# Four RMS norms of a transformer kernel: VectorE adds up the squares, and TensorE's ones product runs on the total

## What the kernel computes

```python
def _rmsnorm(x, g):
    xf = x.astype(jnp.float32)
    y = xf * lax.rsqrt(jnp.mean(xf * xf, -1, keepdims=True) + EPS) * g.astype(jnp.float32)
    return y.astype(x.dtype)

D_MODEL = 1024
SEQ = 512
FFN_HIDDEN = -(-8 * D_MODEL // (3 * 256)) * 256     # 2816
```

## Time and profile before

| | |
|---|---|
| median of 3 runs (lowest, highest) | 3064.34 us (3064.19, 3064.74) |
| span of the profiled execution, first to last instruction | 3059.0 us |
| TensorE busy | 2888.6 us, 94% of the span |
| VectorE busy | 792.2 us, 26% |
| ScalarE busy | 498.4 us, 16% |
| mean granted TensorE clock | 0.974 of full speed |

### The profile page before, as it was taken

The page is one execution under the profiler, slowest core; times in us unless marked ns, Lnnn a source line. Parts: engine busy times, 40 slices in busy tenths (PEclk is TensorE's granted clock), DMA queues, the critical chain, the costliest instruction groups (busy, mean ns, idle before and its releaser), DMA issues. The chain is left out here.

```text
span 3059.0 us, 31313 instructions
## 1 busy us (share of the span) xinstructions
PE 2888.6 (94%) x13580; PEld 1501.2 (49%) x13580; DVE 792.2 (26%) x1577; ACT 498.4 (16%) x1045; POOL 101.0 (3%) x90
## 2 busy tenths in 40 slices
PE   7998999999999999999998999789969989996998
PEld 4343475444455447544446745788623334432332
DVE  2325531010003233000002274555221231112113
ACT  2333310000001231000001231443110010001001
POOL 1000000000010010000000200010000000000000
PEclk9999999999999999999999999998989999997999
DMA  7211036545221111222111201100099953009994
GB/s 244 93 42 42 28 115 262 218 180 220 82 85 69 68 66 56 87 78 83 69 69 60 111 29 59 34 23 2 23 399 419 419 207 145 14 6 395 419 420 193
DMA packets 68577, 430.81 MB, mean 141 GB/s; under 512 B 8042, under 2 KB 8857, under 8 KB 21464
## 3 DMA queue, kind: packets, MB, share of 16 engines
q1 hardware_dynamic: 63640, 412.48, 34.5%
q0 software_dynamic: 4800, 16.33, 1.5%
HBM read 422.33 MB, written 13.79 MB: 143 GB/s over the span
## 5 line engine op out<-in xcount | busy, mean ns | idle before, releaser
L295 PE MATMUL bank<-h,weight_ring 128*128 128x512 f32 (+1 forms) x1600 | 608.3, 542 | 0.0
L295 PEld LDWEIGHTS bank<-h,weight_ring 128*128 128x128 f32 x1600 | 303.1, 190 | 300.3 <-issue 290.4
L254 PE MATMUL bank<-arena,weight_ring 128*128 128x512 f32 (+1 forms) x1264 | 422.9, 491 | 0.0
L254 PEld LDWEIGHTS bank<-arena,weight_ring 128*128 128x128 f32 x1264 | 238.1, 190 | 170.5 <-issue 154.5
L2151 PE MATMUL bank<-weight_ring,tokens_T 128*64 128x512 f32 x1024 | 231.8, 603 | 1.5 <-issue 1.5
L906 PE MATMUL bank<-h,weight_ring 128*128 128x512 f32 (+2 forms) x464 | 183.1, 547 | 5.2 <-DVE h L202 3.4
L2638 PE MATMUL bank<-h,weight_ring 128*128 128x256 f32 (+1 forms) x576 | 172.9, 457 | 8.5 <-ACT h L1933 8.5
L309 DVE TENSOR_TENSOR arena<-bank,arena 128x512 f32<-128x512 f32 (+1 forms) x50 | 31.4, 627 | 557.3 <-ACT arena L304 557.3
L3286 PE MATMUL bank<-h,weight_ring 128*128 128x512 f32 x384 | 166.6, 597 | 3.7 <-DMA weight_ring<-in_sc_in 3.7
L2151 PEld LDWEIGHTS bank<-weight_ring,tokens_T 128*64 128x64 f32 x1024 | 77.0, 139 | 153.0 <-issue 147.6
L2638 PEld LDWEIGHTS bank<-h,weight_ring 128*128 128x128 f32 x576 | 109.5, 192 | 70.6 <-issue 55.9
(11 more groups left out here) (387 smaller groups left out, 2633.0 us busy)
## 6 DMA issues: line engine op xcount, KB each, us to landing
weight_ring<-in_w_gate SPq DMA_DIRECT2D x64, 1024.0 KB, 25.0
weight_ring<-in_w_up SPq DMA_DIRECT2D x64, 1024.0 KB, 26.3
weight_ring<-in_w_down SPq DMA_DIRECT2D x64, 1024.0 KB, 26.1
arena<-in_ada_w SPq DMA_DIRECT2D x48, 1024.0 KB, 9.1
weight_ring<-in_gu SPq DMA_DIRECT2D x44, 1024.0 KB, 4.8
weight_ring<-in_down SPq DMA_DIRECT2D x22, 1024.0 KB, 4.8
weight_ring<-in_sc_in SPq DMA_DIRECT2D x12, 1024.0 KB, 12.2
weight_ring<-in_ev_in SPq DMA_DIRECT2D x8, 1024.0 KB, 6.9
```

Of the source, the lines that this page charges most:

```text
L254: m = pe.matmul(bank, self.slots[i].buf[:, at * P:(at + 1) * P], self.src(c)[:, lo:hi], start=(c == 0), stop=(c == self.kt - 1))
L295: m = pe.matmul(self.k.bank[:, 2 * (u % 2) + p, lo:hi], self.slots[t].buf[:, at:at + P], self.h[:, c, lo:hi], start=(c == 0), stop=(c == K ...
```

## The change

A class `FoldedNorm` takes the place of `Norm` in the four norms. Squares now rotate through three buffers, and the fourth buffer holds a running total. VectorE adds each unit's squares to the total (`add_square`), except for the last unit of each half. TensorE does two ones products for each half: one on the total (`sum_total`) and one on the squares of the half's last unit (`sum_alone`).

```diff
+    def __init__(self, k, name, src, units, ready, gain, dst, banks, temps):
...
+        self.squares, self.total = squares[:, 0:3, :], squares[:, 3, :]
+        self.alone = [max(u for u, (t, i, j) in enumerate(units) if i < hi and j > lo) for lo, hi in SPANS]
+        self.adds = [u for u in range(1, len(units)) if u not in self.alone]
...
+    def square(self, a, u):
+        t, lo, hi = self.units[u]
+        after(a, *self.ready[u])
+        if u >= 3 and u - 3 in self.alone:
+            after(a, self.summed, 2 * self.alone.index(u - 3) + 1)
+        elif u >= 3:
+            after(a, self.added, self.adds.index(max(u - 3, 1)))
...
+    def add_square(self, v, u):
+        t, lo, hi = self.units[u]
+        i = self.adds.index(u)
+        after(v, self.squared, u)
+        if i:
+            after(v, self.added, i - 1)
+        so_far = self.squares[:, 0, lo:hi] if i == 0 else self.total[:, lo:hi]
+        v.tensor_tensor(self.total[:, lo:hi], self.squares[:, u % 3, lo:hi], so_far, ALU.add).then_inc(self.added.sem, 1)
+
+    def sum_total(self, pe, s):
+        lo, hi = SPANS[s]
+        after(pe, self.added, max(i for i, u in enumerate(self.adds) if self.units[u][1] < hi and self.units[u][2] > lo))
+        pe.matmul(self.k.bank[:, self.banks[s], lo:hi], self.k.ones, self.total[:, lo:hi], start=True, stop=False).then_inc(self.summed.sem, 1)
+
+    def sum_alone(self, pe, s):
+        lo, hi = SPANS[s]
+        u = self.alone[s]
+        after(pe, self.squared, u)
...
@@ -1053,21 +1109,16 @@
                     out.unit(pe, 4)
                     out.unit(pe, 5)
-                    for i in range(4):
-                        norm.sum(pe, i)
                     out.unit(pe, 6)
                     out.unit(pe, 7)
-                    norm.sum(pe, 4)
-                    norm.sum(pe, 5)
                     out.unit(pe, 8)
-                    norm.sum(pe, 6)
-                    norm.sum(pe, 7)
+                    norm.sum_total(pe, 0)
+                    norm.sum_alone(pe, 0)
                     for n in range(9, 12):
                         out.unit(pe, n)
-                    for i in range(8, 11):
-                        norm.sum(pe, i)
                     gate.unit(pe, 0)
-                    norm.sum(pe, 11)
+                    norm.sum_total(pe, 1)
+                    norm.sum_alone(pe, 1)
...
                 def down_stage(d, norm, turn):
                     d.unit(pe, 0)
                     turn()
-                    for n in range(1, 10):
+                    for n in range(1, 9):
                         d.unit(pe, n)
-                        norm.sum(pe, n - 1)
+                    norm.sum_total(pe, 0)
+                    norm.sum_alone(pe, 0)
+                    d.unit(pe, 9)
+                    norm.sum_total(pe, 1)
...
@@ -1227,13 +1281,19 @@
                 def mixer_end(out, norm, gate, group):
-                    for i in range(9):
+                    out.add(v, 0)
+                    out.add(v, 1)
+                    for i in range(2, 8):
                         out.add(v, i)
+                        norm.add_square(v, i - 1)
+                    out.add(v, 8)
                     norm.factor(v, 0)
                     for i in range(3):
                         out.add(v, 9 + i)
                         for t in range(3 * i, min(3 * i + 3, KT)):
                             norm.out(v, 0, t)
+                    for i in range(8, 11):
+                        norm.add_square(v, i)
                     gate.multiply(v, 0)
                     norm.factor(v, 1)
...
                 def down_stage(d, norm, add):
-                    for i in range(9):
+                    d.add(v, 0)
+                    add()
+                    d.add(v, 1)
+                    for i in range(2, 8):
                         d.add(v, i)
-                        if i == 0:
-                            add()
+                        norm.add_square(v, i - 1)
+                    d.add(v, 8)
                     norm.factor(v, 0)
+                    norm.add_square(v, 8)
                     for t in range(KT):
                         norm.out(v, 0, t)
                     d.add(v, 9)
```

More of the change, by code:

```diff
@@ L209, in normed, with root @@
             after(pe, self.done, self.tiles + t)
+class FoldedNorm(Norm):
+    def __init__(self, k, name, src, units, ready, gain, dst, banks, temps):
+        self.k, self.src, self.tiles, self.units, self.ready = k, src, KT, units, ready
+        self.gain, self.dst, self.banks = gain, dst, banks
+        squares, self.rms, self.rstd, self.factor_ = temps
+        self.squares, self.total = squares[:, 0:3, :], squares[:, 3, :]
+        self.alone = [max(u for u, (t, i, j) in enumerate(units) if i < hi and j > lo) for lo, hi in SPANS]
+        self.adds = [u for u in range(1, len(units)) if u not in self.alone]
+        self.squared = Turns(k.flag("norm_squared"), len(units))
+        self.added = Turns(k.flag("squares_added"), len(self.adds))
+        self.summed = Turns(k.flag("norm_summed"), 4)
+        self.rooted = Turns(k.flag("norm_rooted"), 2)
+        self.chain = Turns(k.flag("norm_chain"), 10)
+        self.done = Turns(k.flag("norm_done"), 2 * KT)
+    def square(self, a, u):
[5 more added lines that the diff above has]
+            after(a, self.added, self.adds.index(max(u - 3, 1)))
+        a.activation(self.squares[:, u % 3, lo:hi], self.src[:, t, lo:hi], ACT.Square,
+                     scale=(KT * P) ** -0.5).then_inc(self.squared.sem, 1)
+    def add_square(self, v, u):
[14 more added lines that the diff above has]
+        after(pe, self.squared, u)
+        pe.matmul(self.k.bank[:, self.banks[s], lo:hi], self.k.ones, self.squares[:, u % 3, lo:hi],
+                  start=False, stop=True).then_inc(self.summed.sem, 1)
+    def root(self, a, s):
+        lo, hi = SPANS[s]
+        after(a, self.summed, 2 * s + 1)
+        if self.chain.start:
+            a.wait_ge(self.chain.sem, self.chain.start)
+        a.activation(self.rms[:, lo:hi], self.k.bank[:, self.banks[s], lo:hi], ACT.Sqrt, bias=self.k.eps).then_inc(self.rooted.sem, 1)
@@ L805, in first_block, with ffn @@
         norms, gated, down = [], [], []
-        def ffn(out, gain, number, bank_ready):
-            n = Norm(k, "ffn", x, KT, out.units, [(out.added, i) for i in range(12)], gain, h, (7, 6), temps, number)
+        def ffn(out, gain, bank_ready):
+            n = FoldedNorm(k, "ffn", x, out.units, [(out.added, i) for i in range(12)], gain, h, (7, 6), temps)
             g = GatedUnits(k, ring, n, h, hidden, silu)
@@ L820, in first_block @@
                          panels, rows, both, ctx_mod, (out0.added, 11))
-        norm1, gated0, down0 = ffn(out0, vec["norm_ffn0"], 16, {0: [(mod.kept, 10)], 1: [(mod.kept, 11)]})
-        norm2 = Norm(k, "mix1", x, KT, down0.units, [(down0.added, i) for i in range(10)], vec["norm_mix1"], h, (7, 6), temps, 28)
+        norm1, gated0, down0 = ffn(out0, vec["norm_ffn0"], {0: [(mod.kept, 10)], 1: [(mod.kept, 11)]})
+        norm2 = FoldedNorm(k, "mix1", x, down0.units, [(down0.added, i) for i in range(10)], vec["norm_mix1"], h, (7, 6), temps)
         plan = [(f"{n}{t}", "act") for ts in ((0, 1), (2, 3)) for n in ("vin", "u") for t in ts]
@@ L860, in first_block @@
                               2: [(second.biased, scores - 2)], 3: [(second.biased, scores - 1)]})
-        norm3, gated1, down1 = ffn(out1, vec["norm_ffn1"], 38, {})
-        norm4 = Norm(k, "final", x, KT, down1.units, [(down1.added, i) for i in range(10)], vec["final_gain"], x, (7, 6), temps, 50)
+        norm3, gated1, down1 = ffn(out1, vec["norm_ffn1"], {})
+        norm4 = FoldedNorm(k, "final", x, down1.units, [(down1.added, i) for i in range(10)], vec["final_gain"], x, (7, 6), temps)
         def unit_products(pe, p, slots, name, first_c, stop):
@@ L1123, in _ @@
                 unit(pe, proj2, slot2, "vin0")
-                norm2.sum(pe, 9)
+                norm2.sum_alone(pe, 1)
                 for name in proj2.names[1:10]:
@@ L1150, in _ @@
                 down_stage(down1, norm4, lambda: None)
-                norm4.sum(pe, 9)
+                norm4.sum_alone(pe, 1)
             @block.scalar
```

## The result

The changed kernel ran in 3040.73 us (median of 4 runs, 3038.26 to 3042.60), the kernel before in 3064.27 us (4 runs); the ratio is 0.9921 with a 95% interval of 0.9907 to 0.9935. Over all comparisons of this study the changed kernel has 16 runs with a mean of 3042.1 us (standard deviation 2.3), the kernel before 110 runs with a mean of 3064.1 us (standard deviation 2.0): 22.0 us faster, with a 95% interval of +- 1.2 us if the runs are drawn independently.

A forecast was written before the change was run, and what follows sets the result against it. TensorE's gapless product stream was taken to bound the kernel. Span 3059.0 - 20.8 = 3038.2 us, plus 5.3 us from span to median run, gave 3043.5 us; likeliest 3042.5 to 3044.5, range 3041.0 to 3046.5 us.

The forecast's parts named there:

- The ones products: In the four norms, 48 fewer TensorE products at 0.433 us between starts: 5.19 us a norm, 20.8 us in all.
- the rival by weight loads: In the norms, weight loads set the price of a removed product: 18.2 us gained, 3046.1 us; chance 0.04.
- The adds on VectorE and their places: In the norms, 17.9 us of added VectorE work, with slack at every point, so no cost.
- The slack ahead of gate unit 0: In a mixer's norm, the last two scaled tiles are ready 1.6 us before TensorE needs them; it was 2.9.
- The end of the block: After the first block's last unit, the chain to the second block keeps the same parts: no cost or gain.
- the transfers: Loads wait for TensorE, which reaches the slots up to 5.2 us sooner in a norm; no TensorE wait ends on one.
- the clock behind the norms: Rival: in the second block the clock returns sooner or later; gain 18 to 24 us; chance 0.06 beyond the likeliest range.
- The price of the clock's return: At the second block's start, after 8.40 us of idle, TensorE's return from half to full clock costs 2.65 us.
- VectorE was late nowhere: Rival: VectorE late before gate unit 0 or among full tiles, each mixer losing 1 to 2 us; chance 0.07.
- no gain: Rival: in each norm the products only filled TensorE's waiting time; result within 6.1 us of 3064.3; chance 0.02.
- slower: Rival: VectorE's new link delays the lower half, TensorE idles and its clock falls; about 3071 us; chance 0.01.
- not as long as before: Sign of being wrong: the second block, which follows the norms, changes its length; no size given.

The follow-up runs named there:

- adds_only: Kernel before plus 32 more VectorE additions at the new places, into a buffer nobody reads, all ones products kept: 3062.40 us, ratio 0.9995.
- padded: Changed kernel with 48 ones products on a constant tile put back at the old places, VectorE's adds kept: 3061.58 us, ratio 0.9993.
- before_again: The kernel before, unchanged, measured against itself: 3062.84 us, ratio 1.0001.
- all_folded2: Changed kernel with each half's last unit also totalled, except the final norm's upper half, and one product moved behind `vin0`: 3041.63 us, ratio 0.9921.
- late_dve: Changed kernel with four reciprocals of 1.75 us on VectorE in both mixers, ahead of the lower half's last two scaled tiles: 3058.67 us.

## Why the prediction was right, and where it was wrong

**The ones products.** Right to 0.1 us: 20.8 us were forecast, 20.70 us is what the stretch lost, and 24 products give 10.36 us, four more cost 1.71 us, seven less give 3.02 us. The distance between starts was the right price. The two bounds (24.5 us from busy time, 18.2 us from the weight loads) were off by 3.8 and 2.5 us, and the rival by weight loads is refuted.

**The adds on VectorE and their places.** Right. They cost nothing in the stretch (`adds_only`, `padded`). Their durations add up to 19.9 us where I worked out 17.9: a full tile took 0.68 us as assumed but for one of 2.96 us, see below. VectorE's busy time rose by 17.4 us, since instructions that follow each other overlap a little. The slack ahead of gate unit 0 was tested and came out at 1.5 us for 1.6. In the last down stage VectorE waits 1.96 us for unit 9 and not 1.7 us, which costs nothing. One detail of the walk was wrong: not all of ScalarE's squares wait for adds, since in a mixer the square of unit 10 takes the buffer of unit 7 and still waits for a ones product (`square` in the diff). TensorE has no wait that comes from it.

**The end of the block, the transfers.** Right: 10.25 us against 10.23, and no wait on a transfer.

**The step that failed** is the one on the clock behind the norms: "Against it: three runs of the kernel before agree within 0.55 us", with the chance of 0.06 drawn from it. The sum takes 20.8 us off one time and puts the change of everything outside the norms at nothing, and this was the only reason given for it. The rival itself was put at 3040.5 to 3046 us, and the measured 3040.73 us lies within it; the range was cut at 3041.0. The runs show a term of microseconds in its place. 110 runs of the kernel before have a standard deviation of 2.0 us and go from 3060.3 to 3070.5 us, and its second block was 1388.0 to 1395.55 us long in three profiles, by how long the clock was at half. The agreement of the three runs was luck. With such runs a median of four has a standard error of about 1.25 x 2.0 / 2 = 1.25 us, and the difference of two such medians 1.41 times that, 1.8 us. The range should have had this on top of the bounds of the price. Of the 23.5 us between the medians, 20.7 us are the stretch. The other 2.8 us lie outside it; scatter of this size gives such a distance now and then, and the remainder of 1 to 2 us that the edited kernels share may be part of it, whose cause is open. With 16 runs the changed kernel has a median of 3042.5 us, inside the range.

A second step misread the same thing: "The median of the runs stands 5.3 us above the profiled span; with that, 3043.5 us". In the 106 runs of the kernel before that list both numbers, time and span lie 1.7 to 1.9 us apart, and in those of the changed kernel 1.7 to 2.6 us. So some 3.5 of the 5.3 us were scatter: the profiled execution of the kernel before was a short one (second block 1388.0 us). That did not bend the forecast itself, since 3064.34 - 20.8 gives the same 3043.5 us. It hid how wide the scatter is.

The price of the clock's return was a little too high. The 16 records from 1671.00 us take 9.55 us, but 16 such records at full clock take 7.03 us and not 6.9, since the last one's duration counts. The return costs 2.5 us there, not 2.65, and 1.9 us in `before_again` (8.95 us).

**The rivals.** No wait took the place of the products, VectorE was late nowhere, and neither "no gain" nor "slower" began. The second block is "not as long as before" in these two profiles, which I had put down as a sign of being wrong; it isn't one, since it differs by more than that between executions of one kernel.

## What to carry to other kernels

Where an engine's stream has no gaps, the price of an instruction is the distance between starts, and moving a sum from the bound engine to one that is idle for most of the time is worth that price, here to a tenth of a microsecond, as long as each new link is shorter than the work that covers it. Look for the one place where the new result is asked for straight behind its source: there the product must be moved, as `all_folded2` shows.

Compare one stretch of two profiles, from the first instruction that the change touches to the first behind it, before comparing times: here it repeats within 0.1 us in profiles of one kernel whose spans differ by 8.5 us. Take the scatter of a kernel whose clock falls in its waits from many runs; three that agree prove little. And compare a variant with runs of the kernel before on the same chip: their means went from 3063.6 to 3065.4 us from chip to chip.

## What the runs showed of the hardware

One add of VectorE with both inputs in on-chip memory took 2.96 us where its likes take 0.68. It ran beside GpSimd's masking of a table, in the first down stage (timeline of the changed kernel, all engines):

```profile
867.22 7.91 POOL L523 TENSOR_TENSOR arena<-arena,constants 128x1792 f32<-128x1792 f32 x2 [641.43 <-DMA arena<-tables]
872.11 0.69 DVE L324 TENSOR_TENSOR x<-bank,x 128x512 f32<-128x512 f32 x1 [17.59 <-PE bank L310]
872.72 2.96 DVE L246 TENSOR_TENSOR arena<-arena 128x512 f32<-128x512 f32 x1
```

GpSimd's second operation ends at 867.22 + 7.91 = 875.13 us, and the add 0.55 us later at 875.68 us. So it looks as if it stood still until GpSimd was done, and then did its work. It is no accident of one execution: in all twelve profiles with an add at this place, of seven kernels, it took 2.9 to 3.1 us and ended 0.55 or 0.56 us behind GpSimd's operation. The add into `x` just ahead of it, with one input in PSUM, ran at its usual 0.69 us beside the same operation. The Trainium skill ("SBUF — State Buffer", SBUF: two separate sides) says that VectorE with two inputs in on-chip memory and GpSimd take a shared port in turn for whole instructions; the rows agree. It cost nothing here, with 9 to 19 us of cover to the next unit, but I had not looked for it when I moved adds to VectorE.

TensorE's clock fell to half in `late_dve` within the 5.5 us without a product, and the products behind it took 1.8 and 1.5 us longer than at full clock. Behind the 8.4 us of idle ahead of the second block they took 2.5, 1.9 and 2.4 us longer in the three profiles of the kernel before (9.55, 8.95 and 9.47 us against 7.03).
